# The final LayerNorm of a mixture-of-experts layer taken off Pool, with the last expert's rows added in PSUM for two of five chunks

## What is computed

```python
g, idx = lax.top_k(jnp.swapaxes(aff, 1, 2), cap)
xs = jax.vmap(lambda hb, ib: hb[ib])(h, idx)
gu = jnp.einsum('becd,edf->becf', xs, w_gate_up)
gate, up = jnp.split(gu, 2, axis=-1)
y = jnp.einsum('becf,efd->becd', jax.nn.silu(gate) * up, w_down) * g[..., None]
# rows y of all experts are added at their tokens idx: ff
x = layer_norm(ALPHA * x + gate2 * ff, ln2_g, ln2_b)   # (x - mean) * rsqrt(var + eps) * g + b
```

## Time and profile before

| | us |
|---|---|
| median of 3 runs | 1014.58 |
| lowest and highest | 1012.61 and 1015.07 |
| the profiled execution, whole | 1015.87 |
| its span, first to last instruction | 1014.0 |

### The profile page before, as it was taken

How to read it: one execution, slowest core, us unless ns; L and a number is a source line. 1 busy time by engine, 2 the same in 40 slices (tenths; PEclk the granted TensorE clock), 3 DMA queues, 4 the chain that set the end, 5 groups by cost and what they waited for, 6 DMA issues and landing times.

```text
span 1014.0 us, 11533 instructions
## 1 busy us (share of the span) xinstructions
PE 892.1 (88%) x4600; PEld 607.3 (60%) x4600; DVE 773.9 (76%) x761; ACT 566.6 (56%) x556; POOL 207.4 (20%) x137
## 2 busy tenths in 40 slices
PE   4699899888879992789999999999999999999850
PEld 1388896345547881456666666666666666666530
DVE  3757530668775988579999889988999998999826
ACT  1515115754562233467777777777777777777702
POOL 1011302000233103200331132112302320222016
PEclk9899999979889996799999999999999999999975
DMA  8900401732005839799999999999999999999133
GB/s 325 388 35 16 176 1 42 275 108 76 1 2 189 331 135 417 259 366 356 363 383 406 380 375 393 393 378 377 399 400 381 376 394 396 373 398 375 50 90 143
DMA packets 57293, 271.87 MB, mean 268 GB/s; under 512 B 7012, under 2 KB 7256, under 8 KB 40856
## 3 DMA queue, kind: packets, MB, share of 16 engines
q1 hardware_dynamic: 48744, 243.67, 61.6%
q0 software_dynamic: 7056, 22.23, 8.1%
q10 hardware_dynamic: 1440, 5.24, 1.4%
HBM read 257.85 MB, written 13.28 MB: 267 GB/s over the span
## 4 chain that ended last, share of the span: by engine, by line
PE 77%; DVE 9%; DMA 4%; ACT 4%; issue 3%; POOL 2%; SPq 0%; ACTq 0%; POOLq 0%
PE PS L814 22%; PE PS L815 22%; PE PS L816 22%; PE PS L959 2%; DMA ring<-in_w_mod 2%; PE PS L940 2%; DVE WAl L1206 1%; DMA w_qkv<-in_w_in 1%; PE PS L927 1%; PE PS L981 1%; PE PS L1096 1%; PE PS L1107 1%; PE PS L829 1%; PE PS L1033 1%; POOL xt L544 1%
## 5 line engine op out<-in xcount | busy, mean ns | idle before, releaser
L1519 DVE TENSOR_TENSOR Wl<-wr,Wh 128x2048 fp32r<-128x2048 f32 x190 | 432.7, 2290 | 55.9 <-ACT Wh L762 55.9
L762 ACT ACTIVATE Wh<-wr 128x2048 fp32r<-128x2048 f32 x192 | 367.4, 1915 | 73.0 <-PE PS L816 72.9
L814 PE MATMUL PS<-Wh,Xh 128*80 128x512 f32 x512 | 204.0, 398 | 4.0 <-issue 2.9
L816 PE MATMUL PS<-Wl,Xh 128*80 128x512 f32 x512 | 202.4, 395 | 0.0
L815 PE MATMUL PS<-Wh,Xl 128*80 128x512 f32 x512 | 202.3, 395 | 0.0
L509 POOL DMA_INDIRECT acc_scratch<-ysc,idx_u x16 | 80.8, 5050 | 433.2 <-DVE ysc L1547 433.2
L814 PE MATMUL PS<-Wh,HTh 128*80 128x512 f32 x256 | 102.3, 400 | 3.1 <-DVE ysc L1547 3.1
L814 PEld LDWEIGHTS PS<-Wh,Xh 128*80 128x80 f32 x512 | 76.4, 149 | 44.5 <-issue 4.2
L816 PEld LDWEIGHTS PS<-Wl,Xh 128*80 128x80 f32 x512 | 76.5, 149 | 42.7 <-issue 1.2
L815 PE MATMUL PS<-Wh,HTl 128*80 128x512 f32 x256 | 101.1, 395 | 0.0
L816 PE MATMUL PS<-Wl,HTh 128*80 128x512 f32 x256 | 100.8, 394 | 0.0
(11 more groups left out here) (243 smaller groups left out, 1220.0 us busy)
## 6 DMA issues: line engine op xcount, KB each, us to landing
wr<-in_w_gate_up SPq DMA_DIRECT2D x128, 1024.0 KB, 8.2
wr<-in_w_down SPq DMA_DIRECT2D x64, 1024.0 KB, 7.7
ring<-in_w_mod SPq DMA_DIRECT2D x24, 1024.0 KB, 8.6
xt<-in_x_sample ACTq DMA_DIRECT2D x8, 512.0 KB, 7.6
ring<-in_w_in SPq DMA_DIRECT2D x4, 1024.0 KB, 13.6
ring<-in_w_out SPq DMA_DIRECT2D x4, 1024.0 KB, 4.9
w_qkv<-in_w_in SPq DMA_DIRECT2D x4, 768.0 KB, 11.9
h_scratch<-h POOLq DMA_DIRECT2D x5, 512.0 KB, 6.5
```

The lines of the kernel that those rows point to most:

```text
L762: act.activation(Wh[n % NWH][:], wr[s][:], ACT.Copy).then_inc(W_hi, 1)
L814: pe.matmul(out, w[0], x[0], start=first, stop=False)
L816: return pe.matmul(out, w[0], x[1], start=False, stop=last)
L1519: dve.tensor_tensor(Wl[s][:], wr[s][:], Wh[n % NWH][:].bitcast(F32), ALU.subtract).then_inc(W_lo, 1)
```

## The change

The final norm is written anew. Pool has no part in it. Five things differ:

- Pool's last scatter (expert 15) still adds its rows to all tokens in HBM, but chunks 0 and 1 (`FIN_PS`) are loaded before it, when the scatter of expert 14 has landed. Pool's last scatter waits until these two loads are in. For these two chunks TensorE adds the last expert's rows itself: it multiplies the loaded chunk by the identity into PSUM and then a one-hot matrix `hot` (80 slots x 640 tokens: 1 where slot s holds token n) by `ysc`, accumulating. Chunks 2, 3 and 4 are loaded behind the last scatter.
- VectorE makes `hot` by comparing column numbers `iota`, loaded by SP behind the last weights, with the last expert's token numbers `idx_last`. It does so behind the rows of expert 14 and ahead of the last unit's `Wl`.
- The last expert's rows are scaled in two halves of 512 columns, each with a signal of its own.
- VectorE takes the statistics of chunks 0 to 2 (0 and 1 from PSUM). The mean is subtracted together with the gain in one operation, and reciprocal deviation and bias are applied in another; ScalarE gives the square root in between.
- For chunks 3 and 4 (`FIN_ACT`) ScalarE makes the sums by accumulating over a pass: once of the chunk, for the mean, and once of the squares, for the deviation.

The chunks stand in `xf` now, three weight slots and what lies behind them, free when the last expert's gate units 3 to 5 are used. The table of the square root is loaded into ScalarE ahead of the norm. Left out of the diff is only the list of semaphores.

```diff
@@ -85,7 +85,7 @@
 W_AT = 12
 MOD4_AT = (2, 2, 2, 3, 3, 3, 4, 4)
 SUM_AT = (1, 5)
-POOL_LAST = 3
+FIN_PS, FIN_ACT = (0, 1), (3, 4)
 OUT_ORDER = (PC,) + tuple(range(PC))
 W_POOL = 2
 
@@ -160,6 +160,8 @@
     idx_u = tile("idx_u", [SL, NE], U32)
     table_scr = tile("table_scr", [P, 1])
     epsc = tile("epsc", [P, 1])
+    idx_last = tile("idx_last", [SL, 1])
+    fin = tile("fin", [P, 2, 2])
     topv = tile("topv", [NE, SL])
     topi = tile("topi", [NE, SL], U32)
     topf = tile("topf", [NE, SL])
@@ -225,6 +227,11 @@
     Xl = [at(f"Xl{b}", [P, KC, SL], Fz + 8192 + (2 * b + 1) * XB, F32R) for b in range(2)]
     HTh = [at(f"HTh{b}", [P, KC, SL], Fz + 8192 + (4 + 2 * b) * XB, F32R) for b in range(2)]
     HTl = [at(f"HTl{b}", [P, KC, SL], Fz + 8192 + (5 + 2 * b) * XB, F32R) for b in range(2)]
+    XF_SLOT = (GU0[NE - 1] + 3) % NSLOT
+    assert XF_SLOT + 3 <= NSLOT
+    xf = at("xf", [P, CH, D], Dz + 8192 * XF_SLOT)
+    iota = at("iota", [SL, NT], Fz)
+    hot = at("hot", [SL, NT], Fz + 4096)
     ln2g = at("ln2g", [P, D], Fz + 32768)
     ln2b = at("ln2b", [P, D], Fz + 36864)
     G2 = at("G2", [SL, D], Cz)
...
@@ -371,15 +378,17 @@
                 sp.dma_start(wr[s][:].rearrange("p (k n) -> p k n", k=2),
                              w_dn_v[e][:, 2 * k:2 * k + 2, :]).then_inc(w_in_slot[s], 16)
 
-        sp.wait_ge(scattered, 16 * NE)
+        sp.wait_ge(x_t, 2 * (NE - 1))
+        sp.dma_start(iota[:], t["consts"][0:SL, P + 256:]).then_inc(misc_in, 16)
+        sp.wait_ge(W_used, GU0[NE - 1] + 6)
+        sp.wait_ge(scattered, 16 * (NE - 1))
         for c in range(CH):
-            sp.dma_start(xt[:, c, :], acc_dram[c * P:(c + 1) * P, :]).then_inc(acc_in[c], 16)
+            if c == len(FIN_PS):
+                sp.wait_ge(scattered, 16 * NE)
+            sp.dma_start(xf[:, c, :], acc_dram[c * P:(c + 1) * P, :]).then_inc(acc_in[c], 16)
         for c in range(CH):
-            if c < POOL_LAST:
-                sp.wait_ge(y_out_pool, c + 1)
-            else:
-                sp.wait_ge(y_out, c + 1 - POOL_LAST)
-            sp.dma_start(y_s[:, c, :] if c < PC else t["y_prompt"][0], xt[:, c, :]).then_inc(stored, 16)
+            sp.wait_ge(y_out, c + 1)
+            sp.dma_start(y_s[:, c, :] if c < PC else t["y_prompt"][0], xf[:, c, :]).then_inc(stored, 16)
         sp.wait_ge(stored, 16 * CH)
 
 
@@ -469,10 +478,6 @@
                 pool.wait_ge(cat_lo, N_PAIR)
             pool.dma_start(dst[:], src.partition_broadcast(P)).then_inc(done, 16)
 
-        def rstds(c, done):
-            link(pow_mhalf(rstd[:, c:c + 1], mv[:, c, 1:2], 1, 1.0))
-            pool.tensor_scalar(nmr[:, c:c + 1], mv[:, c, 0:1], rstd[:, c:c + 1], -1.0, ALU.mult, ALU.mult).then_inc(done, 1)
-
         def h_store(i):
 
             pool.wait_ge(h_ok, 2 * i + 2)
@@ -503,9 +508,12 @@
 
         def scatter(e):
 
-            pool.wait_ge(y_ok, e + 1)
+            pool.wait_ge(y_ok, e + 1 if e < NE - 1 else NE + 1)
             if e:
                 pool.wait_ge(scattered, 16 * e)
+            if e == NE - 1:
+                for c in FIN_PS:
+                    pool.wait_ge(acc_in[c], 16)
             pool.indirect_dma_start(acc_dram, bass.IndirectOffsetOnAxis(ap=idx_u[:, e:e + 1], axis=0), ysc[e % 2][:], None,
                                     compute_op=ALU.add).then_inc(scattered, 16)
 
@@ -534,14 +542,6 @@
             if e:
                 scatter(e - 1)
         scatter(NE - 1)
-        for c in range(CH):
-            pool.wait_ge(var3_ok, c + 1)
-            rstds(c, rstd3_ok)
-            if 1 <= c <= POOL_LAST:
-                x = xt[:, c - 1, :]
-                pool.wait_ge(gain_ok, c)
-                pool.wait_ge(ln2_in, 32)
-                pool.tensor_tensor(x, x, ln2b[:], ALU.add).then_inc(y_out_pool, 1)
         pool.wait_ge(pool_out, 32)
         pool.wait_ge(hout, 32)
 
@@ -715,9 +715,6 @@
         cat_evac(N_PAIR - 1)
 
 
-        def norm(dst, src, c):
-            return act.activation(dst, src, ACT.Identity, bias=nmr[:, c:c + 1], scale=rstd[:, c:c + 1])
-
         def h2_evac(i):
             for h in range(2):
                 act.wait_ge(x2_t, 2 * i + h + 1)
@@ -802,9 +799,37 @@
                 for h in range(2):
                     if n == GU_END[e] + H_AT[h] + LEAD:
                         h_split(e, h)
-        for c in range(CH):
-            act.wait_ge(rstd3_ok, c + 1)
-            norm(xt[:, c, :], xt[:, c, :], c).then_inc(norm3_ok, 1)
+        act.activation(table_scr[:], epsc[:], ACT.Sqrt)
+        steps = [0]
+
+        def step(ins):
+
+            steps[0] += 1
+            ins.then_inc(act_seq, 1)
+            act.wait_ge(act_seq, steps[0])
+
+        def std3(c):
+            act.wait_ge(var3_ok, c + 1)
+            act.activation(nmr[:, c:c + 1], mv[:, c, 1:2], ACT.Sqrt, bias=epsc[:, 0:1]).then_inc(std3_ok, 1)
+
+        def row_sum(c, i):
+            act.wait_ge(acc_in[c], 16)
+            step(act.activation(xt[:, 3, :], xf[:, c, :], ACT.Copy, accum_out=fin[:, 0, i:i + 1]))
+            step(act.activation(nmr[:, c:c + 1], fin[:, 0, i:i + 1], ACT.Copy, scale=-1.0 / D))
+
+        def row_std(c, i):
+            step(act.activation(xt[:, 3, :], xf[:, c, :], ACT.Square, bias=nmr[:, c:c + 1], accum_out=fin[:, 1, i:i + 1]))
+            act.activation(fin[:, 0, i:i + 1], fin[:, 1, i:i + 1], ACT.Sqrt, bias=epsc[:, 0:1],
+                           scale=1.0 / D).then_inc(std3_ok, 1)
+
+        act.wait_ge(hrow_ok, NE)
+        std3(0)
+        std3(1)
+        row_sum(3, 0)
+        std3(2)
+        row_std(3, 0)
+        row_sum(4, 1)
+        row_std(4, 1)
 
 
     @block.tensor
@@ -1144,6 +1169,18 @@
                 for e_ in range(NE):
                     if n == GU_END[e_] + H_AT[h]:
                         h_transposes(e_, h)
+
+        pe.wait_ge(hrow_ok, NE)
+        for c in FIN_PS:
+            pe.wait_ge(acc_in[c], 16)
+            for h in range(2):
+                pe.matmul(bank(2 * c + h), ident, xf[:, c, 512 * h:512 * h + 512], start=True, stop=False)
+            if c == 0:
+                pe.wait_ge(hot_ok, 1)
+            for h in range(2):
+                pe.wait_ge(y_ok, NE + h)
+                pe.matmul(bank(2 * c + h), hot[:, c * P:(c + 1) * P], ysc[(NE - 1) % 2][:, 512 * h:512 * h + 512],
+                          start=False, stop=True).then_inc(fin_ps, 1)
 
 
     @block.vector
@@ -1510,6 +1547,7 @@
 
         dve.wait_ge(top_t, 1)
         dve.tensor_copy(idx_u[:], bank(7, 0, NE, rows=SL))
+        dve.tensor_copy(idx_last[:], bank(7, NE - 1, NE, rows=SL))
         dve.tensor_copy(g_slot[:], bank(7, 16, 16 + NE, rows=SL)).then_inc(slot_ok, 1)
 
         def split_lo_slot(n):
@@ -1544,8 +1582,16 @@
                 dve.wait_ge(g2_in, 32)
             if e >= 2:
                 dve.wait_ge(scattered, 16 * (e - 1))
-            dve.scalar_tensor_tensor(ysc[e % 2][:], PS[0:SL, 2048:3072], g_slot[:, e:e + 1], G2[:],
-                                     ALU.mult, ALU.mult).then_inc(y_ok, 1)
+            cuts = (0, D) if e < NE - 1 else (0, 512, D)
+            for lo, hi in zip(cuts, cuts[1:]):
+                dve.scalar_tensor_tensor(ysc[e % 2][:, lo:hi], PS[0:SL, 2048 + lo:2048 + hi], g_slot[:, e:e + 1], G2[:, lo:hi],
+                                         ALU.mult, ALU.mult).then_inc(y_ok, 1)
+
+        def one_hot():
+
+            dve.wait_ge(misc_in, 64)
+            dve.wait_ge(x_t, 2 * NE)
+            dve.tensor_scalar(hot[:], iota[:], idx_last[:, 0:1], None, ALU.is_equal).then_inc(hot_ok, 1)
 
         x_lo(0, 0)
         x_lo(0, 1)
@@ -1565,23 +1611,32 @@
                         h_lo_part(e, h)
                 if n == DN_END[e] + LEAD:
                     y_evac(e)
-
-
-        for c in range(CH + 1):
-            if c < CH:
-                dve.wait_ge(acc_in[c], 16)
-                layer_stats(xt[:, c, :], c).then_inc(var3_ok, 1)
-            if c:
-                x = xt[:, c - 1, :]
-                dve.wait_ge(norm3_ok, c)
-                if c == 1:
-                    dve.wait_ge(ln2_in, 32)
-                last = dve.tensor_tensor(x, x, ln2g[:], ALU.mult)
-                if c - 1 < POOL_LAST:
-                    last.then_inc(gain_ok, 1)
-                else:
-                    link(last)
-                    dve.tensor_tensor(x, x, ln2b[:], ALU.add).then_inc(y_out, 1)
+                    if e == NE - 2:
+                        one_hot()
+
+
+        dve.wait_ge(ln2_in, 32)
+        for c in range(CH):
+            x = xf[:, c, :]
+            src = PS[:, 1024 * c:1024 * c + 1024] if c in FIN_PS else x
+            if c not in FIN_ACT:
+                if c not in FIN_PS:
+                    dve.wait_ge(acc_in[c], 16)
+                for h in range(2):
+                    if c in FIN_PS:
+                        dve.wait_ge(fin_ps, 2 * c + h + 1)
+                    last = dve.bn_stats(stats[:, c, h, :], src[:, 512 * h:512 * h + 512])
+                link(last)
```

(16 more changed lines are left out.)

## The result

The changed kernel takes 1001.64 us (median of 4 runs, 1000.0 to 1003.5), the kernel before 1014.83 (4 runs): a ratio of 0.987, 95% interval 0.984 to 0.990. The forecast was 1002.2, in 1000.3 to 1006.1. The profiled execution took 1002.45 us with a span of 1000.6.

The account below looks back on a forecast made before the run. Pool's pace in the final norm was taken to bound the 37.3 us tail behind the matrix work. 12.8 us less, 0.15 more, net 12.6, took the median from 1014.58 to 1002.0, stated as 1002.2, range 1000.3 to 1006.1.

Parts of the forecast that it names:

- Pool sets the pace before: Final norm of the old kernel: Pool paces it at 4.47 us a chunk, 2.34 of it the addition.
- Rows in halves: Last expert's rows on VectorE: scaling in two halves costs 0 to 0.1 us, taken as 0.05.
- Loads of chunks 0 and 1 are covered: Before the last scatter: loads land at 974.7 and 976.0, with 2.3 us of cover before Pool wants to scatter.
- TensorE: Added fp32 matmuls behind the last expert's: start about 976.5, chunk 0 complete at 980.1, chunk 1 at 983.6.
- Statistics from PSUM: VectorE's norm: PSUM reads taken as no dearer, 0.2 us for each of four as upper end; 4.28 us a chunk.
- ScalarE: Sums of chunks 3 and 4: 2.9 to 3.4 us a chunk, chunk 4 ready at 995.1, slightly behind VectorE.
- The end: Last product pair of the norm starts at 995.1 and ends at 997.8, against 1010.57; last store 2.6 us in either.
- The one-hot comparison by width: VectorE's 80x640 comparison ahead of the last weight split: between nothing and 0.83 us, hidden.
- the spread of the runs: Whole kernel's time: runs of before lie 1.3 us around their median, used for the forecast's own range.
- The rivals: Cases against the forecast: scatter delayed 0.08, TensorE clock 0.06, slower than before 0.02, ScalarE or PSUM slower 0.08.
- The one in which VectorE delays the last scatter: Tail: Pool's last scatter issue stretches under VectorE's work, 4.0 us added, median 1006.0; chance 0.08.
- The one on the clock: TensorE's added matmuls run at 1.2 GHz after a gap, 5.9 us more, 1007.9; chance 0.06.

Follow-up runs that it names:

- e1: Changed kernel with all five chunks loaded behind the last scatter and all statistics on VectorE, so only Pool is out: 1011.98 us, ratio 0.998 to the kernel before.
- e4: Changed kernel with the loads of chunks 0 and 1 issued only when the last expert's rows are ready: 1008.82 us in one run, tail 27.6 us.
- e5: Changed kernel with two idle 128x1024 SBUF copies on VectorE while Pool issues the last scatter: tail 21.3 us in one profile.
- e6: Changed kernel with one idle two-input 128x1024 SBUF maximum on VectorE while Pool issues the last scatter: tail 21.6 us in one profile.
- e7: Changed kernel with expert 14's rows scaled ahead of a weight split on VectorE: 1000.33 us, ratio 0.986 to the kernel before.
- e8: e7 with VectorE's last two weight splits waiting until Pool has issued expert 14's scatter: 997.6 us, ratio 0.984 to the kernel before.

## Why the prediction was right, step by step

- *Pool sets the pace before.* Right, and it mattered less than its place in the chain suggests: e1 shows 2.0 us. I took what Pool's addition leaves of the 4.47 us for Pool's work on the root; 0.85 of it is Pool's operation stretched by VectorE's product over it.
- *Rows in halves.* Both done 1.4 us after their start where one operation took 1.29: 0.1 us, the upper end.
- *Loads of chunks 0 and 1 are covered.* Right in the sum, wrong in both terms: the scatter landed after 7.42 us and not 6.8, mostly since the one-hot comparison put more of VectorE's work over its issue (Pool busy 3.65 in place of 3.20), and the loads were quicker (3.3 us for chunk 0 where I had 3.78). Chunk 1 was in at 975.98, forecast 976.0, and that this fits so well is luck. e4 gives the worth of the cover: 6.7 us.
- *TensorE.* First product at 976.46 (976.5), four passes in 1.72 us, chunk 0 complete at 980.06 (980.1). Clock at full.
- *Statistics from PSUM.* No dearer than from SBUF: a pair takes 1.29 us from either. Chunks cost 4.16 us, where I had 4.28. I had counted 0.12 too much per chunk by adding the gap of a dependency that is absent here: in the earlier trace rows the next statistics read what the last product wrote (1.33 us from start to start), in the new norm they don't (1.20).
- *ScalarE.* The passes took 1.05 and 1.14 us, the accumulator reads 0.19, one chunk 2.87 after the other (991.70 to 994.57): just below the low end of my bounds of 2.9 to 3.4. (The terms that I named add up to 3.1 at the low end, not 2.9; what I had not counted is that its short operations overlap: the root of 0.30 us at 991.70 let the next pass start after 0.20.) Chunk 3's load, however, landed at 988.80 and not 988.3, mainly since the scatter took 5.23. The two errors cancel, by luck: chunk 4's deviation was ready at 994.87, forecast 995.1.
- *The end:* 997.57, forecast 997.8. The span shrank by 13.4 us, forecast 12.6: 13.0 in the tail, and 0.4 behind it, where the last store and its wait took 3.0 us and not 3.4.
- *Slips that moved nothing.* The one-hot comparison by width is 0.81 us and not 0.83, and took 0.54. The 1.3 us that I gave as the spread of the runs is the profiled execution's distance from their median; the runs themselves lie from 2.0 us below it to 0.5 above.
- *The rivals.* None came. The one in which VectorE delays the last scatter has a real effect behind it (e5, e6) and the wrong size: I charged the loop's whole 5.44 us for an overlap of 0.4 us. The issue grows by about as long as VectorE's work from SBUF lies over it, and statistics from PSUM, which is what overlapped here, cost nothing. Work from SBUF in the same gap cost 0.4 to 0.7 us of tail, where I had put 4. The one on the clock needed a gap, which e4 made, and cost 1.5 us.

## What to carry to other kernels

When the engine that paces a stage is relieved, work out what the next engine needs for the same stage before counting the gain: here VectorE's was 4.16 us a chunk behind Pool's 4.47. The large part came from starting the stage ahead of the HBM round trip, and that part lives on a cover of 2 us: an edit that brings the stage forward spends the cover first, so shorten what stands in it with the same edit. In these runs a DMA that Pool issues was cheap only while VectorE rested or read statistics from PSUM; if its landing is on the path, let VectorE's deferrable work wait for the issue.

## What the runs showed of the hardware

- Pool's issue of the same scatter-add of 80 rows took 1.39 us with VectorE idle, 2.12 to 2.19 with 1.2 us of VectorE's work on SBUF over it, 3.65 with the one-hot comparison and one weight split (changed kernel) and 5.86 with two splits and the comparison (e7), and the landing moved from 4.9 to 5.3 us after the issue to 5.8 and 5.9, 7.4 and 9.5. A copy and a two-input operation did the same, and 0.43 us of statistics from PSUM did nothing. The Trainium skill, "SBUF — State Buffer", section "Who interferes with whom", says so of copies in the two-port modes, and takes tensor_tensor to leave descriptors alone, marked as inferred. e6's 2.12 us speaks against that inference for this indirect DMA. Whether it is the writing of descriptors that waits, or Pool's reading of the token numbers, no run here separates.
- Pool and VectorE also stretched each other in the norm of the kernel before: a product of VectorE took 2.15 us in place of 1.23 with Pool's addition over its start, and a one-column operation of Pool 1.04 in place of 0.19 with that product over it.
- TensorE's granted clock stayed at full over waits of 1.4 us (e7, e8) and 2.5 us (e7, 1.00 from 972 to 980) and fell in or just behind waits of 3.1 us and 5.3 us (e4). In e4 it fell at the end of the wait and was back at full after the first four passes, which took 3.2 us.
